# One step of a hybrid recurrent decoder on one core: norms by three token groups, scalars of the state space layer beside its x projections, a product program without loops

## What is computed

```python
for i in range(DEPTH):                      # DEPTH = 2
    h = rmsnorm(x, norm_mix_w[i])
    if i % 2 == 0:                          # retention (4 heads) and gated delta rule (4 heads)
        out = hybrid_mixer(h, ...)
    else:                                   # Mamba-2: 32 heads, 4 B/C groups
        out = ssm_mixer(h, ...)
    x = x + out
    x = x + swiglu(rmsnorm(x, norm_ffn_w[i]), w_gate[i], w_up[i], w_down[i])
y = rmsnorm(x, norm_final_w)

def rmsnorm(x, w):
    return x * rsqrt(mean(x * x, axis=-1) + EPS) * w
```

## Time and profile before

| | |
|---|---|
| median of 3 runs | 3636.2 us |
| the profiled execution, its own time | 3643.68 us |
| its span, first to last instruction | 3641.9 us |
| PE busy / PE weight loads busy | 3257.6 us (89%) / 3124.2 us (86%) |
| DVE / ACT / POOL busy | 1662.6 (46%) / 738.8 (20%) / 1215.4 us (33%) |
| mean granted TensorE clock | 0.94 |
| chain that ended last | PE 76%, DVE 11%, issue 7%, ACT 2%, POOL 2%, DMA 1% |

### The profile page before, as it was taken

How to read it: one execution, slowest core, us unless ns; L and a number is a source line. 1 busy time by engine, 2 the same in 40 slices (tenths; PEclk the granted TensorE clock), 3 DMA queues, 4 the chain that set the end, 5 groups by cost and what they waited for, 6 DMA issues and landing times.

```text
span 3641.9 us, 48142 instructions
## 1 busy us (share of the span) xinstructions
PE 3257.6 (89%) x20044; PEld 3124.2 (86%) x20044; DVE 1662.6 (46%) x1798; ACT 738.8 (20%) x1017; POOL 1215.4 (33%) x528
## 2 busy tenths in 40 slices
PE   6989797798869999999977999999997799999996
PEld 6888786687759999999977898898987799999996
DVE  5344555463743222312255776867676422222224
ACT  3212223122321000000022423314142200000001
POOL 2232211020112333333322544546444233333331
PEclk9999897798969999999988999999998899999998
DMA  3111100010011111111111312213131011111111
GB/s 139 60 50 57 39 24 30 19 36 25 18 29 35 47 43 46 47 47 41 47 35 47 105 56 93 79 61 117 53 104 53 30 47 47 47 47 47 47 47 59
DMA packets 75237, 191.21 MB, mean 53 GB/s; under 512 B 20964, under 2 KB 30852, under 8 KB 74888
## 3 DMA queue, kind: packets, MB, share of 16 engines
q1 hardware_dynamic: 47200, 145.80, 12.9%
q10 hardware_dynamic: 27816, 42.11, 3.6%
HBM read 164.07 MB, written 19.59 MB: 50 GB/s over the span
## 4 chain that ended last, share of the span: by engine, by line
PE 76%; DVE 11%; issue 7%; ACT 2%; POOL 2%; DMA 1%; DVEq 0%; SPq 0%; ACTq 0%; POOLq 0%
PE ps_set L484 64%; ACT work L951 2%; PE ps_core L735 1%; PE ps_core L890 1%; PE ps_core L753 1%; PE ps_set L521 1%; DVE work L1529 1%; DVE work L1528 1%; DVE work L1805 1%; PE ps_core L895 1%; DVE work L1826 1%; DVE work L1369 0%; PE ps_core L684 0%; DMA w_raw<-in_w 0%; PE ps_core L787 0%
## 5 line engine op out<-in xcount | busy, mean ns | idle before, releaser
L408 POOL TENSOR_TENSOR w_hi<-w_raw,small 128x1024 fp32r<-128x1024 f32 x230 | 453.1, 1970 | 2248.6 <-PE ps_set L484 2232.1
L484 PE MATMUL ps_set<-h_hi,w_hi 128*128 128x344 f32 x3888 | 861.2, 330 | 79.1 <-DVE h_lo L1380 33.6
L484 PE MATMUL ps_set<-h_lo,w_hi 128*128 128x344 f32 x3888 | 833.0, 323 | 0.0
L484 PE MATMUL ps_set<-h_hi,w_lo 128*128 128x344 f32 x3888 | 828.1, 322 | 0.0
L484 PEld LDWEIGHTS ps_set<-h_hi,w_hi 128*128 128x128 f32 x3888 | 660.6, 191 | 97.4 <-issue 84.8
L484 PEld LDWEIGHTS ps_set<-h_lo,w_hi 128*128 128x128 f32 x3888 | 665.2, 191 | 10.0 <-issue 10.0
L484 PEld LDWEIGHTS ps_set<-h_hi,w_lo 128*128 128x128 f32 x3888 | 655.6, 190 | 0.0
L411 POOL TENSOR_TENSOR w_lo<-w_raw,w_hi 128x1024 fp32r<-128x1024 f32 x230 | 608.8, 2647 | 18.1
L1694 DVE TENSOR_TENSOR work<-work,ps_set 128x1032 f32<-128x1032 f32 x44 | 54.1, 1229 | 828.3 <-PE ps_set L484 828.3
L484 PE MATMUL ps_set<-y_hi,w_hi 128*128 128x344 f32 x1440 | 322.4, 333 | 44.3 <-DVE y_lo L1681 17.7
L1404 DVE TENSOR_TENSOR x<-x,ps_set 128x1032 f32<-128x1032 f32 x176 | 216.3, 1229 | 275.6 <-PE ps_set L484 275.6
(11 more groups left out here) (207 smaller groups left out, 3098.2 us busy)
## 6 DMA issues: line engine op xcount, KB each, us to landing
w_raw<-in_w SPq DMA_DIRECT2D x230, 512.0 KB, 3.6
work<-ssm_cum_rows ACTq DMA_DIRECT2D x32, 512.0 KB, 3.9
sample<-in_ssm_state SPq DMA_DIRECT2D x16, 512.0 KB, 4.2
out_ssm_s<-sample SPq DMA_DIRECT2D x16, 512.0 KB, 2.8
x<-in_x SPq DMA_DIRECT2D x8, 516.0 KB, 8.5
work<-work ACTq DMA_DIRECT2D x16, 258.0 KB, 2.4
out_y<-x ACTq DMA_DIRECT2D x8, 516.0 KB, 3.0
sample<-bc_rows SPq DMA_DIRECT2D x8, 512.0 KB, 5.3
```

The costliest lines, as they stand in the source:

```text
L408: return nc.gpsimd.tensor_tensor(w_hi[:, k, :], w_raw[:, k, :], zeros, ALU.add)
L484: mm = nc.tensor.matmul(out[:, g, 0:TN], w[:, slot, cols], v[:, g * TN:(g + 1) * TN], start=(start and n == 0), stop=(stop and n == 2))
```

## The change

1. **Norms by group.** `norm` becomes `boundary`. The output products ahead of norms 1 to 4 go group by group (344 columns), two x tiles a job (`pair_outputs`); the ones ahead of norm 3 do so for the last four x tiles. Per group ACT squares 4 tiles at once (1376 columns, two instructions), DVE folds them in two adds (1376 and 688 columns), PE sums with 2 matmuls into `ps_core`, ACT takes Ln and Exp of 344 columns, DVE and ACT make h and its parts for 8 tiles of 344 columns, and PE runs the first two units' products of that group, one unit after the other. The three groups are interleaved by hand. Norm 0 and the loads of x, norm 4 and the stores of y go by group as well (6 DMAs of 4 tiles x 344 columns each way in place of 8 of 1032 columns; stores move from ACT's queue to SP's).
2. **Scalars beside x.** x0 is projected in norm 2's boundary beside the scalars' unit, x1 to x3 before the scalars' transposes on PE, B and C behind them. DVE convolves x0 between; from the next tile on ACT's copies stand in its queue behind the scalars.
3. **No loops on PE.** All `Fori` on PE are written out; DVE's and ACT's delta loops too.
4. Small moves: the last delta outputs of both turns take the pair form, the convolution states are stored after the norms, the first group's x tiles alternate between two raw slots.

On PE, and where the program calls it:

```diff
+            def group_products(out, slot, block, rhs, g, start, stop):
+                for n, (w, v) in enumerate(((w_hi, hi), (w_hi, lo), (w_lo, hi))):
+                    mm = nc.tensor.matmul(out[:, 0:TN], w[:, slot, cols], v[:, span(g)],
+                                          start=(start and n == 0), stop=(stop and n == 2))
...
+            def boundary(n, outputs_of, first):
...
+                def projections(g):
+                    for jobs, job, unit in first:
...
+                        for c in range(KC):
+                            pe.wait_ge(*norm_dve[n].value(f"lo{c}.{g}"))
+                            mm = group_products(...)
+                        if g == TG - 1:
+                            mm.then_inc(unit_done, 1)
+                outputs_of(0)
+                outputs_of(1)
+                mean_square(0)
+                outputs_of(2)
+                mean_square(1)
+                projections(0)
+                mean_square(2)
+                projections(1)
+                projections(2)
...
-                with pe.Fori(0, (PAIRS - 1) // 2) as i:
+                for i in range((PAIRS - 1) // 2):
...
-            norm(2)
-            scalars(1, SSMS)
-            for name in FRONT:
+            boundary(2, lambda g: ffn_outputs(0, FFN0, g),
+                     [(big_jobs["ssms"], "sc", SSMS), (big_jobs["ssm"], "x0.0", SSM_UNIT["x0", 0])])
+            for name in FRONT[1:4]:
+                fill(projection(name, 0), KC)
+            scalars(1, SSMS)
+            for name in FRONT[4:]:
                 fill(projection(name, 0), KC)
```

ACT's part, in its order:

```diff
+            def boundary(n):
...
+                squares(0)
...
+                squares(1)
+                root(0)
+                squares(2)
+                highs(0)
+                root(1)
+                highs(1)
+                root(2)
+                highs(2)
```

and DVE's, where `adds(g, hf)` are the two adds of half a group and `scaled` makes h and its low part:

```diff
+            def boundary(n, add):
...
+                adds(0, 0)
+                adds(0, 1)
+                adds(1, 0)
+                sums(0)
+                adds(1, 1)
+                adds(2, 0)
+                sums(1)
+                adds(2, 1)
+                scaled(0)
+                sums(2)
+                scaled(1)
+                scaled(2)
```

More of the change, by code:

```diff
@@ L399, in _ @@
             sp.wait_ge(state_out[2], GROUPS * 64)
+            for g in range(TG):
+                for hf in range(2):
+                    tiles = slice(4 * hf, 4 * hf + 4)
+                    sp.wait_ge(*end_dve.value(f"y{g}.{4 * hf + 3}"))
+                    sp.dma_start(o["y"][:, tiles, span(g)], x[:, tiles, span(g)]).then_inc(stored, 16)
+            sp.wait_ge(stored, 16 * 2 * TG)
         @block.gpsimd
@@ L492, in slices, with pair_outputs @@
+            def pair_outputs(jobs, job, turn, slot, blocks, rhs, g, done):
+                part = take(jobs, job, turn)
+                for t, row in enumerate(blocks):
+                    for c, block in enumerate(row):
+                        mm = group_products(ps_set[part][:, t, :], slot, block, rhs[c], g, c == 0, c == len(row) - 1)
+                mm.then_inc(*((unit_done, 1) if done else (part_done, 1)))
+            def slices(jobs, job, turn, unit, slot):
                 part = take(jobs, job, turn)
@@ L501, in slices, with tile @@
                     yield
-            def tile(jobs, job, turn, unit, slot, norm=None):
-                for _ in slices(jobs, job, turn, unit, slot, norm):
+            def tile(jobs, job, turn, unit, slot):
+                for _ in slices(jobs, job, turn, unit, slot):
                     pass
@@ L523, in over_tokens @@
                 return mm
-            def norm(n):
-                jobs = big_jobs[f"norm{n}"]
-                part = take(jobs, "ms")
-                pe.wait_ge(*norm_dve.value(f"sum{KC - 1}", n))
-                over_tokens(part, ones, tok(2)).then_inc(*norm_pe.step("ms"))
-            def together(tiles):
-                for _ in zip(*tiles, strict=True):
-                    pass
             def scalars(layer, unit):
@@ L826, in ffn @@
             def ffn(m, base):
-                first, loop, end = (big_jobs[f"ffn{m}{s}"] for s in ("a", "", "z"))
+                first, loop = (big_jobs[f"ffn{m}{s}"] for s in ("a", ""))
                 def outs(jobs, names, turn, unit, slot, pair):
@@ L924, in _ @@
             pe.wait_ge(consts_in, 48)
-            norm(0)
-            with pe.Fori(0, 2) as i:
+            for i in range(2):
                 retention(i, 0)
@@ L1013, in scalars @@
+                act.wait_ge(*sc_dve[layer].value("a"))
+                act.wait_ge(*sc_act[layer].value("b"))
+                act.dma_start(rows[layer], rs(10)).then_inc(sc_rows, 16)
+                if layer:
+                    raw(1, 0)
+                    silu(0, 0)
+                    raw(2, 0)
                 for hf in range(2):
-                    act.wait_ge(*sc_pe.value(f"row{hf}", layer))
+                    act.wait_ge(*sc_pe[layer].value(f"row{hf}"))
                     fn(tok(11, hf * 512, hf * 512 + 512)[0:heads], ps_core[core.part(f"row{hf}")][0:heads, :], ACT.Copy)\
@@ L1324, in _ @@
             scalars(0, GDNS)
-            with act.Fori(0, 2) as i:
+            for i in range(2):
                 gated_delta(i, 0)
                 gated_delta(i, 1)
+            boundary(1)
             act.dma_start(o["gdn_conv_s"], conv_s[:, 0:12, 1:4, :]).then_inc(conv_out, 16)
@@ new lines, in boundary, with add_pair @@
+                sums(0)
[7 more added lines that the diff above has]
+                scaled(2)
+            def add_pair(jobs, job, turn, g, q, done):
+                dve.wait_ge(*done)
+                part = x[:, 2 * q:2 * q + 2, span(g)]
+                v.tensor_tensor(part, part, ps_set[jobs.part(job)][:, 0:2, 0:TN], ALU.add).then_inc(jobs.sem(job), 1)
@@ L1712, in ffn @@
                         low(1, i * 2 + (k + 1))
-                for t in range(KC):
-                    add_outputs(end, [f"out{t}"], 0, base + 6 * PAIRS - 2, parts + 6 * (PAIRS - 1), t)
-                    if t > 1:
-                        square_sum((2, 4)[m], t - 1)
             def front_tile(k, gr):
@@ L1858, in state_space @@
                 dve.wait_ge(*ssm_act.value(n("rstd")))
[L1859 removed]
+                for t in range(KC if gr + 1 < GROUPS else 4):
                     scaled(t)
```

393 lines of the change are left out of this document (252 added, 141 removed).

## The result

The changed kernel takes 3553.75 us, the median of 4 runs (3553.64 to 3557.07), against 3639.38 (4 runs of before beside it): ratio 0.9771, 95% interval 0.9756 to 0.9786. The forecast was 3575, range 3540 to 3610. The sign and the range held; the gain is 86 us where 61 were forecast. What follows asks where the other 25 came from. The trace of before that all readings use is of an execution of 3643.68 us, the slowest of the 28 executions of that kernel on record (the others took 3623.31 to 3642.71; where their mean granted clock is noted, it is 0.942 to 0.949, and the traced one had 0.940). A comparison of traces therefore gives before a few us more, in clock, than a comparison of medians.

What follows compares the result with a forecast made beforehand. PE's order bounds the kernel (89% busy, 76% of the chain), so time is won only where PE rests. Norms -31.7, loops -26.8, registers -5, clock +3: about -61 us, median 3575, range 3540 to 3610.

Steps and rivals of the forecast that it cites:

- The norms: Norms 0 to 3 and the end, done by group: +1 -8.5 -8.7 -11.7 -3.8, together -31.7 us.
- the template: Each norm, from the first group's root being ready to the next tile: 36.0 us, 4.4 slower than before.
- What stands ahead of the root: At each norm, the work before the first group's root was to give the gain, as the stretch after it got slower.
- The 21.94 us rest: PE's rest before the scalars' transposes after norm 2: covered, mostly given back as about 14 before C; stretch -8.7 us.
- Loops on PE, the FFN: Both FFNs without back edges on PE come to 570.3 us for four turns: -17.2 and -4.6.
- The second turns of retention and delta lose 2.14 and 2.15: PE's rests at those loop heads, and 0.8 after, were to go with the back edges: -5 us.
- Rival A: PE's back-edge rests are waits under another name and stay in straight code: 3602 us; chance 10%.
- Register work, -5: Semaphore-value instructions removed from PE, DVE and ACT, mostly in the delta part: -5 us, from 0 to -30.
- Clock, +3: PE now rests within each norm too; half-clock restarts cost 1.5 us each, six in four norms, most inside rests: +3.
- Rival C: Half clock in the norms' group passes: products end at about 43, not 35, four times 8, 3607 us; chance 5%.
- State space turns, nothing: The three state space turns: forecast difference 0 us.
- Rival D: PE's written-out program gets instructions too late some 160 times at 1.15 us: slower, 3759 us; chance 3%.

Runs made afterwards that it cites:

- scalars_first: The changed kernel with the scalars' transposes ahead of x1 to x3 on PE, ACT's queue to match; 3572.98 us, norm 2's stretch 167.5 for 159.7.
- after_again: The changed kernel executed again with nothing edited; 3550.9 us, ratio 0.9772 to the kernel before.
- tot_first: The changed kernel with ACT's two exponentials of the totals moved ahead of the scalars' DMA issues; 3553.26 us, norm 2's stretch 151.2, 8.6 less.

## Why the prediction was right, and where it was wrong

- **The norms**: right. Sum -27.8 for -31.7. Norm 0 was 1.7 too cheap (root at 26.2, forecast 25.5, and the template 36.9 for 36.0); norm 3 gave 2.2 less, of which 1.65 is a rest for the second output unit's split, which the text did not have.
- **"What stands ahead of the root" gives the gain, the template costs**: right, with the period at 10.8 to 11.0.
- **The 21.94 us rest is covered and most is given back**: right (-7.9 for -8.7; scalars_first +7.8), with the rest at 14.69. Its cause was only half right.
- **Loops on PE, the FFN**: right in kind, short by 5.6 in size (-27.4 for -21.8). The windows of the earlier trace rows ended at the last back edge, so the half clock behind that one was left out, and the 570.3 us taken as the floor held some itself (704.6 us for 4464 products in the change is 568.2 for 3600).
- **"The second turns of retention and delta lose 2.14 and 2.15"**: read rightly, and both rests go with the jump, but in retention that is worth nothing. The 0.8 noted behind it was POOL's split of k, which ends at the same time with or without the jump, so the wait for it grew to 3.13. It left only because the change also reads q and k one after the other there, and that line of the change was not costed at all. Rival A is not what happened, since no rest kept its place under another name, but its result, nothing gained by straight code, held at this one place.
- **Register work, -5**: the step that failed most. No direct worth can be seen (585 to 588 us without half clock), and half clock in the delta rule fell by 19, 11 of them with the step from PE's loops to all loops.
- **Clock, +3**: wrong in sign. More rests were expected to mean more half clock. Half clock fell from 129.1 to 86.1 instead: 19.1 of it in the delta rule, for a reason that stays open, 8.3 in the FFNs, where the rests at the loops' heads went, and 7.5 in the state space turns by luck. Rival C did not come: norm 1's stretch has 4.1 us of half clock for 6.0.
- **State space turns, nothing**: right, since their work did not change and their rests hardly did (2.90 to about 2.55); the first trace gained 7.5 by where half clock fell, and after_again gave 6.6 back. That the gain between the traces, 89.9, is so far above the forecast is in part luck.
- **Rival D**, straight code that starves PE: refuted. FFN 0 in straight code is 704.6 busy of 710.1, and the queue of instructions moved less than before:

```profile
q8 instruction: 159, 2.61, 0.3%
```

So of the 29 us beyond the forecast between the traces (25 between the medians) about 9 are in the delta rule, 7.5 in retention, 5.6 in the FFNs, and 8, not to be counted on, in the turns, less 4 that the norms and norm 0 fell short, with the +3 that did not come.

## What to carry to other kernels

Sum the busy time of PE times one minus its granted clock, stretch by stretch, before costing anything: here it was 129 us of 3642, and it moves when a short wait inside a dense stretch goes. Before a rest at a loop's head is counted as a gain, look at the next wait behind it: if another engine ends its work at the same time either way, that wait grows by what the rest gave (0.76 to 3.13 us here). And judge an edit of under 10 us by its own stretch in the trace; its total can be hidden (tot_first) or doubled (scalars_first) by half clock elsewhere.

## What the runs showed of the hardware that was not expected

- One program, two executions: the same rest (2.54 and 2.55 us) was followed by full clock in one and by 1.7 us of half clock cost in the other; a rest of 2.83 by none. Over thirteen traces, rests of 1.85 us were followed by half clock in 25 of 51 cases, of 2.5 to 2.85 in 23 of 32, of 2.89 to 3.10 in 7 of 7.
- Writing out ACT's and DVE's loops raised the granted clock of PE over 34 us of the same recurrence from 0.50 to 0.80 (0.75 in the change).
- A DVE sum of two 688-column operands took 0.88 us alone and 2.45 beside a split on POOL.
